# State space tiles: normalization sums ahead of the next products with scores, outputs turned ahead of the segment sums

## The reference

```
acum = cumsum(dt * a_neg)                                  # per head
decay_ls = where(causal, exp(acum[l] - acum[s]), 0)        # the segment sums
cb = einsum('bclgn,bcsgn->bclsg', cc, bc)                  # C against B
y_intra = einsum('bclsg,bclsgh,bcsghp->bclghp', cb, decay_ls, xd)
chunk_states = einsum('bclgn,bclgh,bclghp->bcghpn', bc, to_end, xd)
s = s * chunk_decay + chunk_states                         # from block to block
y_inter = einsum('bclgn,bcghpn,bclgh->bclghp', cc, s_in, exp(acum))
y = y_intra + y_inter + d_skip * xs
y = y * silu(z)
out = group_rms_norm(y, norm_w, 2)                         # mean of squares over 512 channels
```

## Time and profile before

| | us |
|---|---|
| median of 3 runs (4209.46 to 4215.49) | 4212.96 |
| the profiled execution | 4210.1 |
| its span, first to last instruction | 4208.0 |
| the state space phase in it | about 1098 to 1340 |
| TensorE busy, of the span | 3762.5 (89%) |
| VectorE busy | 1568.2 (37%) |
| ScalarE busy | 729.5 (17%) |
| GpSimd busy | 998.3 (24%) |
| mean granted TensorE clock | 0.934 |

### The profile page before, as it was taken

One profiled execution on the slowest core, in us unless ns is written; L12 is line 12 of the kernel. 1 busy time (PEld: TensorE's weight loads), 2 busy tenths in 40 slices (PEclk: granted clock), 3 DMA queues, 4 the chain that ended last, 5 costly groups with the idle time before them and its releaser, 6 DMA issues. The chain is left out here.

```text
span 4208.0 us, 65631 instructions
## 1 busy us (share of the span) xinstructions
PE 3762.5 (89%) x28016; PEld 3541.8 (84%) x28016; DVE 1568.2 (37%) x2095; ACT 729.5 (17%) x1150; POOL 998.3 (24%) x824
## 2 busy tenths in 40 slices
PE   4699986888786989999999899979987799999997
PEld 1399985776564979999999799978877799999997
DVE  0341344664565452222222602007763622222225
ACT  0111124442432010000000116104431100000001
POOL 3322222110001332322323323230002322222221
PEclk9899997997786989999999899999987899999998
DMA  9522222100422111111111123223332111111111
GB/s 351 207 91 90 85 80 38 29 20 2 100 51 70 42 31 40 46 37 49 41 36 45 33 87 128 94 84 86 76 90 66 35 38 48 37 46 43 35 45 60
DMA packets 379805, 285.32 MB, mean 68 GB/s; under 512 B 17795, under 2 KB 361345, under 8 KB 373486
## 3 DMA queue, kind: packets, MB, share of 16 engines
q1 hardware_dynamic: 362240, 232.55, 18.8%
q10 hardware_dynamic: 17262, 50.23, 3.1%
q0 software_dynamic: 128, 0.00, 0.2%
HBM read 223.47 MB, written 59.29 MB: 67 GB/s over the span
## 5 line engine op out<-in xcount | busy, mean ns | idle before, releaser
L514 PE MATMUL ffn_acc<-hH,ffn_wH 128*128 128x384 f32 x2112 | 712.4, 337 | 28.3 <-DVE hL L437 28.3
L514 PE MATMUL ffn_acc<-hL,ffn_wH 128*128 128x384 f32 x2112 | 710.1, 336 | 0.0
L514 PE MATMUL ffn_acc<-hH,ffn_wL 128*128 128x384 f32 x2112 | 485.4, 336 | 0.0
L497 POOL CAST ffn_wH<-ffn_raw 128x1024 fp32r<-128x1024 f32 (+2 forms) x168 | 145.5, 866 | 1204.6 <-PE ffn_acc L514 1158.5
L514 PEld LDWEIGHTS ffn_acc<-hH,ffn_wH 128*128 128x128 f32 x2112 | 399.7, 189 | 35.7 <-DVE hL L437 18.4
L514 PEld LDWEIGHTS ffn_acc<-hL,ffn_wH 128*128 128x128 f32 x2112 | 400.2, 189 | 0.0
L514 PEld LDWEIGHTS ffn_acc<-hH,ffn_wL 128*128 128x128 f32 x2112 | 379.9, 189 | 0.0
L1048 DVE TENSOR_TENSOR ffn_norm_m<-ffn_acc,ffn_norm_m 128x1152 f32<-128x1152 f32 x44 | 59.7, 1358 | 858.0 <-PE ffn_acc L514 858.0
L514 PE MATMUL ffn_acc<-ffn_uH,ffn_wH 128*128 128x384 f32 x1056 | 352.7, 334 | 0.0
L514 PE MATMUL ffn_acc<-ffn_uL,ffn_wH 128*128 128x384 f32 x1056 | 352.7, 334 | 0.0
L499 POOL TENSOR_TENSOR ffn_wL<-ffn_raw,ffn_wH 128x1024 fp32r<-128x1024 f32 (+2 forms) x168 | 323.1, 1923 | 13.5
(11 more groups left out here) (506 smaller groups left out, 6477.3 us busy)
## 6 DMA issues: line engine op xcount, KB each, us to landing
pro_w<-in_ada_w SPq DMA_DIRECT2D x24, 2048.0 KB, 17.9
ffn_raw<-in_w_gate SPq DMA_DIRECT2D x44, 512.0 KB, 3.9
ffn_raw<-in_w_up SPq DMA_DIRECT2D x44, 512.0 KB
pT<-in_ab_out ACTq DMA_DIRECT2D x34, 576.0 KB, 3.0
pT<-in_c_out ACTq DMA_DIRECT2D x32, 576.0 KB, 3.0
in_ab_raw<-in_w_in_ab SPq DMA_DIRECT2D x34, 512.0 KB, 3.8
in_c_raw<-in_w_in_c SPq DMA_DIRECT2D x32, 512.0 KB, 4.2
hgrn_kqg<-pT SPq DMA_DIRECT2D x9, 1536.0 KB, 8.9
```

What stands on the lines that cost most here:

```text
L497: nc.gpsimd.tensor_copy(wH, raw).then_inc(self.hi_half[u], 1)
L514: ins = nc.tensor.matmul(self.acc[0:rows, u, c, 0:CH], w[:, u, k, 0:rows], x[:, k, c * CH:(c + 1) * CH], start=(k == 0 and w is self.wH an ...
```

## The change

Orders within a step and the waits that go with them. TensorE sums the squares of tile t - 1 ahead of intra(t), not behind it; turns the outputs and forms the state ahead of the segment sums, and does all four of these in a row. The sums of squares go to bank 0 (bank 3 for the last tile as before), so `square_sum` waits for the exponentials of the tile's segment sums and the next `segments(u, 0)` for the root. VectorE does `finish(t - 1)` between y1 and y2, and `scale_state` behind `skip`. ScalarE spreads the decays in two halves, with the root between them, and `RL_done` counts halves.

```diff
@@ -2260,6 +2261,7 @@
         by_head = lambda ap: ap.rearrange("p (h q) -> p h q", q=HDB)
         by_tile = lambda ap: ap.rearrange("p (j c) -> p j c", c=P)
         heads = lambda i: slice(GH * i, GH * i + GH)
+        sums_at = lambda t: 0 if t < LAST else 3
 
         @block.sync
         def _(sp):
@@ -2278,11 +2280,11 @@
         def _(act):
             nc.scalar.preload_act_table_set("natural_log_exp_and_others")
 
-            def spread_decays(u):
+            def spread_decays(u, half):
                 if u:
                     act.wait_ge(seg_mm, 4 * u)
                 mask = g.notafter if u == LAST else g.notafter128
-                for h in range(HB):
+                for h in range(half * GH, half * GH + GH):
                     ins = nc.scalar.activation(RL[:, h, :], mask[:, :], ACT.Identity, scale=decays.tok[:, 1, u, h:h + 1])
                 ins.then_inc(RL_done, 1)
 
@@ -2307,7 +2309,7 @@
                 act.wait_ge(ss_mm, t + 1)
                 if t:
                     act.wait_ge(out_done, t)
-                nc.scalar.activation(rs[:, :, :].rearrange("p g c -> p (g c)"), bank[:, 3, 0:256], ACT.Ln,
+                nc.scalar.activation(rs[:, :, :].rearrange("p g c -> p (g c)"), bank[:, sums_at(t), 0:256], ACT.Ln,
                                      bias=g.eps[:, 1:2], scale=1.0 / (WB // 2)).then_inc(var_ln, 1)
                 act.wait_ge(var_ln, t + 1)
                 nc.scalar.activation(rs[:, :, :], rs[:, :, :], ACT.Exp, scale=-0.5).then_inc(rs_done, 1)
@@ -2315,10 +2317,11 @@
             for t in range(-1, NT + 1):
                 u = t + 1
                 if u <= LAST:
-                    spread_decays(u)
+                    spread_decays(u, 0)
                 if 1 <= t:
                     root(t - 1)
                 if u <= LAST:
+                    spread_decays(u, 1)
                     take_seg(u, 0)
                     take_seg(u, 1)
                     take_B(u)
@@ -2454,19 +2457,19 @@
                 u, mid = t + 1, 0 <= t <= LAST
                 if mid:
                     inter(t)
+                if 1 <= t:
+                    finish(t - 1)
+                if mid:
                     intra(t)
                     if t == LAST:
                         split_rows()
                 if u <= LAST:
                     weigh(u)
                     mask_CB(u)
-                if mid and t < LAST:
-                    scale_state(t)
-                if 0 <= t - 1:
-                    finish(t - 1)
                 if mid:
                     skip(t)
                 if mid and t < LAST:
+                    scale_state(t)
                     add_state(t)
                 if mid:
                     gate(t)
@@ -2485,8 +2488,6 @@
             def inter(t):
                 pe.wait_ge(CB_done, t + 1)
                 pe.wait_ge(B_out, t + 1)
-                if t >= 2:
-                    pe.wait_ge(var_ln, t - 1)
                 if t < LAST:
                     pe.wait_ge(S_done, t + 1)
                     for i in range(2):
@@ -2531,8 +2532,10 @@
                 ins.then_inc(CB_mm, 1)
 
             def segments(u, i):
-                if i == 0:
-                    pe.wait_ge(RL_done, u + 1)
+                if i % 2 == 0:
+                    pe.wait_ge(RL_done, 2 * u + i // 2 + 1)
+                if i == 0 and u >= 2:
+                    pe.wait_ge(var_ln, u - 1)
                 n = 4 * u + i - 1
                 if n > 0:
                     pe.wait_ge(seg_out, n)
@@ -2558,6 +2561,7 @@
                 pe.wait_ge(xde_split, 1)
                 pe.wait_ge(S_done, NTP + 1)
                 pe.wait_ge(seg_out, 4 * NT)
+                pe.wait_ge(var_ln, LAST)
                 for b in range(NS):
                     if b >= 2:
                         pe.wait_ge(S_done, NTP + 1 + b - 1)
@@ -2569,10 +2573,13 @@
 
             def square_sum(t):
                 pe.wait_ge(sq_done, t + 1)
-                pe.wait_ge(y1_done, min(t + 2, NT))
+                if t < LAST:
+                    pe.wait_ge(seg_out, 4 * (t + 2))
+                else:
+                    pe.wait_ge(y1_done, NT)
                 for i in range(2):
                     for j in range(4):
-                        ins = mm(bank[:, 3, i * P:(i + 1) * P], g.ones[:, :], squares(t)[:, 4 * i + j, :],
+                        ins = mm(bank[:, sums_at(t), i * P:(i + 1) * P], g.ones[:, :], squares(t)[:, 4 * i + j, :],
                                  start=(j == 0), stop=(j == 3))
                 ins.then_inc(ss_mm, 1)
 
@@ -2580,21 +2587,20 @@
                 u, mid, front = t + 1, 0 <= t <= LAST, t + 1 <= LAST
                 if mid:
                     inter(t)
-                    intra(t)
                 if 1 <= t:
                     square_sum(t - 1)
+                if mid:
+                    intra(t)
                 if front:
                     turn_x(u)
                     grams(u)
-                    segments(u, 0)
-                    segments(u, 1)
                 if mid:
                     turn_y(t)
                     if t < LAST:
                         state(t)
                 if front:
-                    segments(u, 2)
-                    segments(u, 3)
+                    for i in range(4):
+                        segments(u, i)
                 if t == LAST:
                     sequence_states()
```

## The result

The changed kernel took 4165.8 us (median of 4 runs, 4162.7 to 4168.1), the kernel before, run again beside it, 4212.5. The ratio is 0.9889, its 95% interval 0.9872 to 0.9906: 46.7 us, 1.1%. The profiled execution has a span of 4166.0 us where it was 4208.0.

The account below looks back on a forecast made before the run. TensorE and VectorE taking turns, with holes that drop TensorE's clock, bound the tiles. Intra(8) 53.3 us earlier less 3.3 lost in the last tile: 50 off 4210.1, 4160, said as 4162 by the median; range 4150 to 4172.

Parts of the forecast that it names:

- The clock: TensorE in the state space tiles: with its idle holes closed, granted clock 1.00 throughout; a tile gains 3.8 to 8.6 us.
- The row on transposes: Profile row 1340.9 to 1344.2: TensorE did only transposes at 0.50, then the clock rose to 1.00, against the page's rule.
- The ring: Tile loop through TensorE and VectorE, intra to intra: 15.58 us after the change, 19.38 at full clock before.
- The slim margins inside the ring: Spare time inside a tile: finish under intra 0.3 us, last exponential before the scores 0.7, sums of squares 0.1.
- The sums, and finish: Sums of squares (1.84 us) go into the hole ahead of intra; finish (2.29 us) hides under intra, 0.3 to spare.
- turn_y, the segment sums, scale_state: Reordering within a tile: skip starts without a wait, segment sums hidden by 0.7 us, scale_state costs the same.
- The load of x: SP queue, behind z: lands 6.2 us after issue, 6.6 at most; hidden barely, 0.9 us counted once in the second tile.
- the first rival: A transfer or ScalarE replaces the wait: late by 1.4 us per tile, ring 17.0, 4171 us; chance 0.15.
- the forecast's own signs of being wrong: Intra 7 us in several tiles, weigh waiting for the load in the ring, or finish(7) under 5 us.
- Intra(8): Start of the last tile's intra: 1240.2 us where it was 1293.5, so 53.3 us earlier.
- The tail: Last tile, after intra(8): finish(7) slowed beside POOL's scaling, y2 15.5 us after intra(8); loss 3.3, bounds gain 5, loss 6.
- The sum: Whole phase: 53.3 us earlier at intra(8) less 3.3 in the last tile gives 50, all reaching the end.

Follow-up runs that it names:

- the fills: Kernel before, plus constant products or transposes in TensorE's holes: 4191.5 us (products ahead of intra), 4200.2 (transposes there), 4186.2 (products in both holes).
- the fill with transposes: Kernel before, with 16 transposes of a constant between inter and intra in tiles 0 to 7: 4200.2 us, ratio 0.9964.
- the other half: Changed kernel with the old orders of turn_y, segment sums and scale_state; sums of squares and finish stay moved: 4162.0 us, ratio 0.9882.
- where finish stays: Changed kernel with finish put back behind mask_CB on VectorE, sums of squares still ahead of intra: 4177.6 us, ratio 0.9918.

## Why the prediction was right, and where its terms were off

The time came out at 4165.8 for 4162, in the range, by the mechanism foreseen: the holes closed, the clock kept, finish and the sums off the ring. That it came so near is in part luck: a fall and late loads in the ring and a loss in the tail that did not come nearly cancel.

- *The clock.* Right: every intra at 3.8 us, and 1.00 in all of the stretch but the 3.3 us behind the late load. What was an inference then, that the holes pull the clock down, the fills show. One reading was wrong: not each fall comes behind two holes. Inter(1), the row below, starts without one, so the first fall (intra at 1128.88) has only the 2.50 us before it; the last (1293.52), too, has only 2.62. The row on transposes pointed the right way against the rule of that page of the Trainium skill; the fill with transposes bears it out in this kernel.

```profile
1124.42 1.96 PE L2493 MATMUL mamba_bank<-mb_S,mamba_xbc 128*128 128x512 f32 x4
```

- *The ring.* 15.58 forecast, 15.76 measured. The slim margins inside the ring held, finish 0.58 us of it. The 0.18 is the term for scale_state, counted at 1.13 in its new place: add_state now stands right behind it and starts 1.32 us after it.
- *The sums, and finish.* The forecast ring takes 3.80 off 19.38, of which finish is 2.29 and so the rest 1.5; measured 2.29 and, for the sums with the new order of the turns, 1.33.
- *turn_y, the segment sums, scale_state.* Costed at nothing but the fit; 0.08 us per tile beside the other half, and nothing that the time shows without it.
- *The load of x.* "Hidden, barely" was wrong in two tiles beyond the one counted: waits of 0.89 (counted), 0.91 and 0.26 us. The median landing was 7.0 us in the changed kernel (the list of DMA issues), 7.6 at most, not 6.2 and 6.6, and the second wait brought a clock fall with it: that ring was 18.20, 2.4 over the others. This was the first rival at a small size, and one of the forecast's own signs of being wrong; the kernel with x ahead of z in the queue prices it at 3.35 us in all. I had taken the row's 6.6 as the most it could be.
- *Intra(8).* 53.3 us earlier was forecast; counted from intra(0), 49.4 measured. The 3.94 us between them: 0.96 from the first five rings and the seventh, 2.62 from the ring of 18.20, 0.36 from the last one (17.56 for 17.2).
- *The tail.* A loss of 3.3 was forecast, none came (the terms as written, 15.5 + 1.2 + 1.7 + 6.8, give 25.2 and a loss of 3.0). The mechanism is there: six of the eight operations of finish(7) at 1.98 us. But finish ended at 13.9 us after intra(8), not 15.5 (one operation took 1.05 us and the last 0.34), and the samples' sums ran without a break, 22.46 us where 6.8 for the first two and the 17.37 that the other six took before make 24.2. That the tail is as long as before is an accident: turn_y starts 5.0 us later after intra(8) (15.15 for 10.12), and the samples' sums, from their first product to the next operation, are 5.0 shorter (22.39 for 27.41, which held the 6.41 us hole). That this place could give 10 us back was not seen: I priced the collision without asking whether it had to be.
- *The sum.* 50 forecast in the phase, 49.4 measured there; 42.0 in the span of the two profiled executions and 46.7 between the medians. In that pair the rest lies in other phases, 3.4 us ahead of intra(0) and 4.0 behind the start of the write of the states; I take it for scatter and have not followed it further.

## What to carry to other kernels

Where TensorE's clock falls inside a loop, look first for its holes: here moving work of another tile into them paid twice, and filling all of them with useless products told how much of it is the clock. Take an operation off the ring only after naming what it then lies beside: finish was free under intra in seven tiles and six times as long beside GpSimd in the last. A margin of 0.4 us on a load whose landing varies by 1.5 us (6.1 to 7.6 here) is no margin.

## What the runs showed of the hardware

- Products of constants in TensorE's holes sped the kernel up by 0.5 to 0.7% (ratios 0.9946 and 0.9934).
- The length of a hole alone did not decide whether the clock fell. All behind intra, it fell behind one of 0.91 us and held behind one of 0.89 in the same kernel and behind 1.18 and 1.09 where finish stays.
- The clock stayed at 0.50 through 24.3 us of TensorE work without a break, of which 22.46 are the samples' sums, products over 32 partitions (the changed kernel):

```profile
1262.70:1287.00 24.30, 24.30 (x41) 10.10 (x41) 13.20 (x18) 1.06 (x1) 0.00 (x0) 0.50 0.00 0
```

- Eight scalar-tensor-tensors of 128 columns (0.34 us each alone) took 12.75 us beside GpSimd's tensor-tensors of 1.9 us: six of them took 1.98 us, about one GpSimd operation each. With GpSimd held back, VectorE's tensor-tensor that reads PSUM beside SBUF was not slowed by it (L2455, 1.21 to 1.22 us beside GpSimd), and gate, which reads two SBUF tensors, took 2.04 us for 1.22.
